# Experts' token lists from rank 3 on: from matrix products in every pass to one scatter through DRAM

## The reference, cut to what matters

```python
top_logit, top_e = lax.top_k(logits, 4)              # logits = rmsnorm(h) @ w_router + b_router
gates = softmax(top_logit)
for each expert e, on the tokens that chose it:
    gate, up = split(x @ w_gate_up[e] + b_gate_up[e])
    act = (clip(up, -7, 7) + 1) * min(gate, 7) * sigmoid(1.702 * min(gate, 7))
    y = act @ w_down[e] + b_down[e]
h = h + sum over the four experts of gates * y
```

## Time and profile before

| | us |
|---|---|
| median of three runs | 2447.67 (2446.9 to 2454.19) |
| the profiled execution | 2456.49 |
| its span, first to last instruction | 2454.7 |
| the 32 passes of the experts | 773.0 to about 2304 |
| one pass, 192 columns / 108 columns | 63.5 / 43.3 |
| PE / DVE / ACT / POOL busy | 2378.4 / 1148.4 / 586.3 / 349.0 |

### The profile page before, as it was taken

The page is one execution under the profiler, slowest core; times in us unless marked ns, Lnnn a source line. Parts: engine busy times, 40 slices in busy tenths (PEclk is TensorE's granted clock), DMA queues, the critical chain, the costliest instruction groups (busy, mean ns, idle before and its releaser), DMA issues. The chain is left out here.

```text
span 2454.7 us, 48279 instructions
## 1 busy us (share of the span) xinstructions
PE 2378.4 (97%) x19277; PEld 2186.8 (89%) x19278; DVE 1148.4 (47%) x1886; ACT 586.3 (24%) x1248; POOL 349.0 (14%) x371
## 2 busy tenths in 40 slices
PE   8999999989996999999999999999999999999898
PEld 6787787688675999999999999999999999999776
DVE  4686816575435223334333434435434334343485
ACT  4434414644321000011011111111111111111265
POOL 0240103262001000110001100101001010010230
PEclk9999996999998999999999999999999999999899
DMA  4131214001526766778888888888888988888652
GB/s 154 66 125 56 95 56 148 27 3 32 193 69 238 285 231 234 249 259 282 288 288 280 296 305 304 304 323 302 315 326 312 321 311 320 313 310 305 211 202 77
DMA packets 123451, 541.02 MB, mean 220 GB/s; under 512 B 15301, under 2 KB 47257, under 8 KB 74169
## 3 DMA queue, kind: packets, MB, share of 16 engines
q1 hardware_dynamic: 106904, 487.45, 56.0%
q0 software_dynamic: 16416, 51.66, 6.2%
HBM read 492.13 MB, written 46.92 MB: 220 GB/s over the span
## 5 line engine op out<-in xcount | busy, mean ns | idle before, releaser
L1960 PE MATMUL ex_psum<-ex_xT,weight_ring_a 128*128 128x134 f32 (+14 forms) x7168 | 896.8, 286 | 4.2 <-DVE ex_xT L1813 3.5
L1960 PEld LDWEIGHTS ex_psum<-ex_xT,weight_ring_a 128*128 128x128 f32 x7168 | 882.0, 191 | 5.0 <-issue 4.3
L2002 PE MATMUL ex_psum<-ex_hT,weight_ring_b 128*128 128x134 f32 (+14 forms) x4096 | 506.0, 286 | 0.0
L2002 PEld LDWEIGHTS ex_psum<-ex_hT,weight_ring_b 128*128 128x128 f32 x4096 | 503.0, 191 | 0.0
L1799 POOL DMA_INDIRECT ex_rows<-xn_dram,ex_list x164 | 155.4, 948 | 1358.9 <-DVE ex_list L1855 1311.7
L1970 DVE TENSOR_SCALAR ex_gate<-ex_psum,bias_gate_up 128x192 f32<-128x192 f32 x256 | 92.6, 403 | 521.4 <-PE ex_psum L1960 515.8
L1974 DVE TENSOR_SCALAR ex_up<-ex_psum,bias_gate_up 128x192 f32<-128x192 f32 x256 | 94.9, 413 | 388.9 <-PE ex_psum L1960 235.7
L1987 ACT ACTIVATE ex_sig<-ex_gate 128x384 f32<-128x384 f32 x128 | 67.0, 523 | 765.8 <-DVE ex_gate L1970 726.9
L2012 ACT ACTIVATE ex_yT<-ex_psum,bias_down 128x192 f32<-128x192 f32 x256 | 83.1, 436 | 503.3 <-PE ex_psum L2002 503.3
L2265 PE MATMUL project_psum<-n_hi,w_in_hi 128*128 128x512 f32 x464 | 186.0, 401 | 2.9 <-DVE n_lo L541 2.9
L2265 PE MATMUL project_psum<-n_lo,w_in_hi 128*128 128x512 f32 x464 | 182.1, 392 | 0.0
(11 more groups left out here) (358 smaller groups left out, 2489.3 us busy)
## 6 DMA issues: line engine op xcount, KB each, us to landing
weight_ring_a<-in_w_gate_up SPq DMA_DIRECT2D x224, 1024.0 KB, 4.8
weight_ring_b<-in_w_down SPq DMA_DIRECT2D x128, 1024.0 KB, 7.1
weight_ring_b<-in_w_gate_up SPq DMA_DIRECT2D x32, 1024.0 KB, 6.9
y_dram<-ex_y SPq DMA_DIRECT2D x80, 192.0 KB
w_in_pieces<-in_w_in SPq DMA_DIRECT2D x29, 512.0 KB, 3.6
y_dram<-ex_y SPq DMA_DIRECT2D x52, 128.0 KB
distances_dram<-qkvT POOLq DMA_DIRECT2D x12, 512.0 KB, 3.0
gla_dist<-distances_dram SPq DMA_DIRECT2D x12, 512.0 KB, 4.3
```

The source lines that it names most:

```text
L1960: mm = pe.matmul(self.ps[:, bank, i * CAP:i * CAP + width], w[:, k, i * P:(i + 1) * P], self.xT[:, k, 0:width], start=(k == 0), stop=(k == ...
L2002: mm = pe.matmul(self.ps[:, bank, first:first + width], w[:, i, j], self.hT[:, k, 0:width], start=(k == 0 and j % 2 == 0), stop=(k == KT - ...
```

## The change

The lists of ranks 0, 1 and 2 (`FIRST_LISTS` = 3) are made as before. For the others:

- `dve_slots` moves to before pass 1. The slot of a token and choice holds its rank and its place.
- A new DRAM tensor `list_dram` has one number per slot. SP zeroes its first part from the blank tile, between the wait for `y_zero` and the store of the blank rows. DVE waits for that zeroing (`lists_zero`) before pass 0, and POOL before its first scatter.
- POOL scatters for each of 8 token tiles and 4 choices 128 numbers (four times the token's number, a constant) to the slots: 32 indirect DMAs. The first 16 stand behind the gather for rank 1, then comes the gather for rank 2, then the other 16, then a wait for all of them and four reads of the whole table with one rank per partition.
- DVE waits for these reads before pass 2 and turns them (`dve_turn_lists`). In each pass from 2 on, a small DVE instruction (`dve_list_by_rank`) takes the place of `dve_list`.
- PE, from pass 2 on, has no list and no fold; DVE has no marks and no spread.
- The loops of the passes are cut at 2 on PE, and into six stretches in place of four on DVE.
- The extra passes for experts with over 192 tokens keep the old way. They are entered only where a count exceeds the capacity.

```diff
+FIRST_LISTS = 3
...
+    k[:, K_ROW:K_ROW + NT] = QUARTERS * (np.arange(NT) * P + i[:, None])
...
+    def dve_list_by_rank(self, dve, x, narrow=False):
+
+        n = BLOCKS_NARROW if narrow else BLOCKS
+        with self.nc.allow_low_precision(reason="row numbers, whole numbers below 2**24"):
+            dve.tensor_scalar(self.list[:, 0:n], self.lists[:, 0:n, bass.ds(x, 1)].rearrange("p b a -> p (b a)"),
+                              self.g.k[:, K_QUARTER:K_QUARTER + 1], None, ALU.add).then_inc(self.listed, 1)
+
+    def pool_scatter(self, pool, tiles):
+
+        g = self.g
+        for t in tiles:
+            for k in range(TOPK):
+                pool.indirect_dma_start(out=g.list_dram, out_offset=bass.IndirectOffsetOnAxis(ap=g.slot[:, t, k:k + 1], axis=0),
+                                        in_=g.k[:, K_ROW + t:K_ROW + t + 1], in_offset=None).then_inc(self.scattered, 16)
+
+    def pool_read_lists(self, pool):
+
+        g = self.g
+        pool.wait_ge(self.scattered, 16 * NT * TOPK)
+        for a in range(QUARTERS):
+            pool.dma_start(self.by_rank[a * SQ:(a + 1) * SQ, :],
+                           g.list_dram[CAP:CAP + E * CAP, :].rearrange("(e n) a -> e (n a)", n=CAP)).then_inc(self.lists_in, 16)
+
+    def dve_turn_lists(self, dve):
+        dve.wait_ge(self.lists_in, 16 * QUARTERS)
+        dve.wait_ge(self.last_zero, 1)
+        dve.transpose(self.lists[:, :, 0:E], self.by_rank[:].rearrange("p (b r) -> p b r", r=SQ)).then_inc(self.lists_turned, 1)
+        dve.wait_ge(self.lists_turned, 1)
...
             sp.wait_ge(x.y_zero, 1)
+            sp.dma_start(g.list_dram[0:Y_FIRST, :].rearrange("(e n) a -> e (n a)", n=CAP),
+                         x.y[0:E + 1].rearrange("p b r -> p (b r)")[:, 0:CAP]).then_inc(x.lists_zero, 16)
...
             x.first_gather(pool)
-            with pool.Fori(0, NARROW - 1) as e:
+            x.gather(pool, 1)
+            pool.wait_ge(x.lists_zero, 16)
+            pool.wait_ge(x.slot_done, 1)
+            x.pool_scatter(pool, range(NT // 2))
+            x.gather(pool, 2)
+            x.pool_scatter(pool, range(NT // 2, NT))
+            x.pool_read_lists(pool)
+            with pool.Fori(2, NARROW - 1) as e:
...
                 for c in range(4):
                     x.pe_gate_up(pe, e, e + 1, c, width)
-                    if c == 0:
-                        x.pe_list(pe, e + 1, 8 * e + 4, narrow_x)
-                    if c == 1:
-                        x.pe_fold(pe, e + 1, narrow_x)
+                    if marks and c == 0:
+                        x.pe_list(pe, e + 1, 8 * e + 4)
+                    if marks and c == 1:
+                        x.pe_fold(pe, e + 1, e + 1)
...
             x.dve_fit(dve)
-            for first, end in ((0, NARROW - 1), (NARROW - 1, NARROW), (NARROW, NARROW + 1), (NARROW + 1, E)):
-                narrow = first + 1 >= NARROW
-                if first == NARROW - 1:
+            dve.memset(x.lists[:, :, E:E + 1], 0.0).then_inc(x.last_zero, 1)
+            dve.wait_ge(x.lists_zero, 16)
+            for first, end in ((0, 1), (1, FIRST_LISTS - 1), (FIRST_LISTS - 1, NARROW - 1), (NARROW - 1, NARROW), (NARROW, NARROW + 1), (NARROW + 1, E)):
+                narrow, marks = first + 1 >= NARROW, first + 1 < FIRST_LISTS
+                if first == 1:
                     x.dve_slots(dve)
+                if first == FIRST_LISTS - 1:
+                    x.dve_turn_lists(dve)
                 with dve.Fori(first, end) as e:
-                    x.dve_find(dve, e + 1, x.expert_at(dve, e + 1, E))
+                    if marks:
+                        x.dve_find(dve, e + 1, x.expert_at(dve, e + 1, E))
...
                         if c == 1:
-                            x.dve_list(dve, e + 1, None, narrow)
+                            if marks:
+                                x.dve_list(dve, e + 1, None)
+                            else:
+                                x.dve_list_by_rank(dve, e + 1, narrow)
```

More of the change, by code:

```diff
@@ L1745, in __init__ @@
         self.list = sb("list", [P, BLOCKS], U32)
+        self.by_rank = sb("lists_by_rank", [P, CAP])
+        self.lists = sb("lists", [P, BLOCKS, E + 1])
         self.spread_a = sb("spread_a", [P, 2, BLOCKS_NARROW], BF16)
@@ L1766, in __init__ @@
         self.y_zero, self.banks_zero = sem("y_zero"), sem("banks_zero")
+        self.lists_zero, self.scattered, self.lists_in, self.lists_turned, self.last_zero = (
+            sem(n) for n in ("lists_zeroed", "lists_scattered", "lists_in", "lists_turned", "last_list_zero"))
         self.first_rows = [sem(f"first_rows_in{b}") for b in range(BLOCKS)]
@@ L1814, in dve_first_turns, with pe_list @@
         turn.then_inc(self.x_turned, 1)
-    def pe_list(self, pe, x, kept, narrow=False):
-        pe.wait_ge(self.marked, x + 1)
-        pe.wait_ge(self.spread, 2 * x)
+    def pe_list(self, pe, i, kept, narrow=False):
+        pe.wait_ge(self.marked, i + 1)
+        pe.wait_ge(self.spread, 2 * i)
         pe.wait_ge(self.yT_kept, kept)
@@ L1824, in pe_list, with dve_spread @@
         mm.then_inc(self.list_summed, 1)
-    def dve_spread(self, dve, x, narrow=False):
-        dve.wait_ge(self.list_summed, x + 1)
-        dve.wait_ge(self.folded, x)
+    def dve_spread(self, dve, i, narrow=False):
+        dve.wait_ge(self.list_summed, i + 1)
+        dve.wait_ge(self.folded, i)
         block = self.g.k[:, K_BLOCK:K_BLOCK + BLOCKS_NARROW]
@@ L1836, in dve_spread, with pe_fold @@
                               self.ps[0:n, self.LIST, 2:4].unsqueeze(2).to_broadcast([n, 2, more]), ALU.mult).then_inc(self.spread, 1)
-    def pe_fold(self, pe, x, narrow=False):
-        pe.wait_ge(self.spread, 2 * x + 2)
+    def pe_fold(self, pe, i, x, narrow=False):
+        pe.wait_ge(self.spread, 2 * i + 2)
         pe.wait_ge(self.listed, x)
@@ L1846, in pe_fold, with dve_list @@
         mm.then_inc(self.folded, 1)
-    def dve_list(self, dve, x, landed, narrow=False):
-        dve.wait_ge(self.folded, x + 1)
+    def dve_list_by_rank(self, dve, x, narrow=False):
[20 more added lines that the diff above has]
+        dve.wait_ge(self.lists_turned, 1)
+    def dve_list(self, dve, i, landed, narrow=False):
+        dve.wait_ge(self.folded, i + 1)
         if landed is not None:
@@ L2162, in passes @@
             def passes(first, end, columns):
-                cuts = sorted({first, end} | {c for c in (NARROW - 1,) if first < c < end})
+                cuts = sorted({first, end} | {c for c in (FIRST_LISTS - 1,) if first < c < end})
                 for lo, hi in zip(cuts, cuts[1:]):
                     if hi == lo + 1:
-                        one_pass(lo, columns, lo + 1 >= NARROW)
+                        one_pass(lo, columns, lo + 1 < FIRST_LISTS)
                     else:
                         with pe.Fori(lo, hi) as e:
-                            one_pass(e, columns, lo + 1 >= NARROW)
+                            one_pass(e, columns, lo + 1 < FIRST_LISTS)
             first = 0
@@ L2227, in _ @@
                         x.dve_gate_up(dve, e, expert, c)
-                        if c == 0:
-                            x.dve_spread(dve, e + 1, narrow)
+                        if marks and c == 0:
+                            x.dve_spread(dve, e + 1)
                         if c == 1:
-                            x.dve_list(dve, e + 1, None, narrow)
+                            if marks:
+                                x.dve_list(dve, e + 1, None)
+                            else:
+                                x.dve_list_by_rank(dve, e + 1, narrow)
                         if c == 2:
@@ L2239, in body @@
                 expert = x.expert_at(dve, e)
-                x.dve_find(dve, n + E + 1, expert)
-                x.dve_spread(dve, n + E + 1)
-                x.dve_list(dve, n + E + 1, x.rows_total_late(n) - 16 * BLOCKS)
+                x.dve_find(dve, n + FIRST_LISTS, expert)
+                x.dve_spread(dve, n + FIRST_LISTS)
+                x.dve_list(dve, n + FIRST_LISTS, x.rows_total_late(n) - 16 * BLOCKS)
                 x.dve_turn_x(dve, n + E + 1, x.rows_total_late(n), 8 * m)
```

16 lines of the change are left out of this document (9 added, 7 removed).

## The result

| | us | runs |
|---|---|---|
| kernel after, median | 2432.37 (2431.79 to 2436.77) | 5 |
| kernel before beside it | 2447.96 (2446.9 to 2454.19) | 5 |
| after / before | 0.9939, 95% interval 0.9926 to 0.9952 | |
| profiled execution of after, its span | 2432.29, 2430.5 | 1 |

The kernel became 0.6% faster, 14.9 us by the ratio (11.8 to 18.1). The forecast was 2432.0.

The account below looks back on a forecast made before the run. PE's queue was taken as the bound (busy 97%). Removed lists 26.0 us, less 7.6 of stall and 2.7 of clock, gave 15.7 off the 2447.67 median: 2432.0 us, range 2420 to 2445.

Parts of the forecast that it names:

- The removal: PE, passes 2 to 31: list matmuls of ranks 3 to 32 go, a gain of 26.0 us.
- The steps for passes 2 to 12: PE, passes 2 to 12: the list costs 1.06 us a pass, 11.7 us in all.
- the late ones: PE, the 14 passes with the narrow list: 0.37 us a pass, 5.2 us in all.
- I let it go together with the list: PE, passes 13 to 17: issue stops vanish with the list, 1.83 us a pass, 9.15 us in all.
- the lower bound: Smallest gain from removing the lists on PE, if the issue stops of passes 13 to 17 stay: 22.2 us.
- The stop in pass 0: PE at the rank 1 list stands still while DVE waits for the zeroing: 7.6 us, bounds 3.2 to 9.5.
- The clock behind it: PE after the stall in pass 0: 5.4 us at half speed, a loss of 2.7 us, bounds 0 to 4.7.
- Slots and marks on DVE: DVE: slot computation (7.3 us) before pass 1 fits idle time, dropped marks were under cover; no cost or gain.
- The scatters: POOL: 32 scatters at 1.25 us each and four reads, lists landing at 910.3, 17.7 us spare; no cost.
- rival C: POOL: scatters to DRAM are slow; from 2.7 us each the whole gain is gone, 2463.6 us at 3.2; chance 0.12.
- A: Pass 0: the zeroing lands in time, no stall and no clock loss, 2421.7 us; chance 0.10.
- B: Pass 0: blank rows hold up the zeroing until about 798, a 17.6 us stall, 2442.0 us; chance 0.12.

Follow-up runs that it names:

- e10: The kernel before, unchanged, profiled once more in one run: 2449.67 us.
- e3: Kernel after with all its additions kept, but every list still made by marks and matrix products, the scattered lists unused: 2456.26 us, 1.0023 of the kernel before.
- e1: Kernel after with DVE's wait for the zeroing moved to its first write into the blank tile: 2426.41 us, 0.9906 of the kernel before.
- e2: Kernel after with SP issuing the zeroing ahead of the four 1024 KB loads: 2424.28 us, 0.9896 of the kernel before.
- e4: Kernel after plus 16 + 4 small one-shape matmuls of constants in passes 2 to 31, without DVE: 2455.41 us, 1.002 of the kernel before.
- e6: Kernel after with all 32 scatters undivided, ahead of rank 2's gather: 2435.53 us, 0.994 of the kernel before.
- e5: Kernel after with every scatter issued twice, the second into an unread table, 64 in all: 2448.83 us, 1.0001 of the kernel before.
- e11: Kernel after plus small matmuls of constants in the wide list's shapes, passes 2 to 31; 2394.53 us, no measure because a slip narrowed the big matmuls.
- e9: Kernel after with both the zeroing issued ahead of the loads and DVE's wait for it made later: 2427.89 us, 0.9909 of the kernel before.
- e8: Kernel before with only the slot computation moved from before pass 18 to before pass 1: 2450.8 us, 0.9999 of the kernel before.

## Why the prediction was right

**What bounds the kernel.** Right: PE's queue set the time. 24.2 us went from span to span: 27.2 in passes 1 to 31, less 7.5 that came back in pass 0. The rest, 4.5, lies almost all ahead of pass 0, which began at 773.0 before and at 768.9 after; without any change it began at 769.3 in e10, so this part is not a gain of the change.

**The removal: the term that was mis-sized.** The steps for passes 2 to 12 (1.06; 1.08 measured) and for the late ones (0.37; 0.40) held. The one that failed is "I let it go together with the list", for the stops of passes 13 to 17. They did go in after, but e3 and e10 show that they had belonged to the one execution of before that was profiled: without a change passes 1 to 31 take 1464.1 us in e10 and 1468.4 in the earlier trace rows's execution, and 1441.2 in after. The change is worth 22.9 us there, not 26.0: the 9.15 us booked for these five passes were 5.4. The 22.2 of the lower bound was nearer. Why the stops were there once is open.

**The stop in pass 0.** The mechanism was right, as e1, e2 and e3 show from three sides. Its size was forecast at 7.6 us; it was 4.09, 4.40, 5.83, 5.83, 8.07 and 8.09 in the six profiled executions that have it, median 5.83. Two things made the difference. Where chunk 0 ran at half clock (after, e4 and e6), PE came 1.7 us later and stood that much less: with a chunk 0 at full clock the stops of after, e6 and e5 would be 5.8 to 6.1 us, those of e4, e3 and e11 7.5 to 8.1. And in these last three the packets of the zeroing end with three late ones, 1.3 to 2.2 us behind the other 30, while in the first three all 33 come within 1 us. After's own stop had both the slow chunk and no late packet: its zeroing had landed by about 782, over 1 us before the load ahead of it, where I had put it 0.9 behind.

The Trainium skill (DMA: Bandwidth & Descriptors, Why a DMA increments its semaphore by 16 and not by 1) states that a transfer from SP uses the largest number of engines, up to 16, that divides its outer dimension, 11 for 33 rows, and that the semaphore is complete when these have landed their data. The traces fit this: in all six executions the last packet of the zeroing ends before the load ahead of it has landed, by 0.2 to 2.5 us, and the three late packets are as many as one of 11 engines would have. No view names a packet's engine, so that isn't shown. The 4.5 us that the prediction worked out by it was nearer to after's 4.09; its own 7.6 was nearer to the stops with late packets.

**The clock behind it.** Forecast 2.7 us lost. Half of the time that PE worked at half clock behind the stop is 1.7 us in after, 1.8 in e3, and at most 3.4 (e11, its stop 8.09), with a median of 2.8: inside the bounds. After 4.09 us of standing still at granted 1.00 the clock was 0.50 for 3.4 us; behind e5's 10.16 us it was 0.50 for 3.57.

**Stop and clock together** were booked at 10.3 us. In the six executions they are 5.8 to 11.5, median 8.9. Pass 0 as a whole, which also holds a slow chunk 0, has a median of 72.95 us in these six and of 65.01 in the seven profiled executions without the stop: 7.9 us. By the ratios of e1, e2 and e9 it is 8.1, 10.5 and 7.4, by that of e3 5.6. So the loss was probably smaller than booked, by some 2 us, though the intervals of e1, e2 and e9 don't exclude the full 10.3; that of e3 (3.2 to 8.1) does.

**Slots and marks on DVE: nothing.** Right within the noise: e8 measured 0.9999 (0.9986 to 1.0012), pass 1 took 63.48 us as before, and 11.24 us of idle time were left.

**The scatters: nothing.** 1.27 us each against 1.25 taken. Their last landed 8.00 us after POOL was through with it, not 2.9, but the four reads took 2.09 us of POOL and not 5.0, the stage began 4 us earlier, and the stop was shorter: turned at 907.66 against a landing forecast at 910.3. The room was 12.9 us and not 17.7. e5 showed the wait behind it where the prediction put it, and that rival C's way of losing the gain is real: with twice the scatters the gain is gone.

**The rivals.** A (no stop) is what e1, e2 and e9 are, and not what after is: 2424.3 to 2427.9 there against A's 2421.7. B (blank rows hold the zeroing up to 798) fell: it had landed by 782. C fell by the scatter's 0.97 us and 0.30 to the next.

**The sum.** 26.0 - 10.3 = 15.7 was booked. By the profiles it is 22.9 - 8.9 = 14.0, or 15.0 with the 7.9 of pass 0 as a whole; the ratio gives 14.9 (11.8 to 18.1). Removal and loss were both taken too high, by 3.1 and by 1.4 to 2.4 us, and this cancelled for the most part: that the sum came so near owes something to luck.

## What to carry to other kernels

A small transfer that an engine waits for belongs ahead of the large ones in its queue, or its wait as late as its data is needed: here that made the gain half as large again or more (0.6% became 0.9 to 1.0% in e1, e2 and e9). A stop seen in one profiled execution is no property of the kernel: before a term is taken from it, look for it in a second execution. And work moved to an engine off the path is free only up to its slack; doubling it, as e5 does, measures both the slack and the price beyond.

## What the runs showed of the hardware

- Small bf16 matmuls of 2 columns with one shape follow each other at 25 ns (16 in 0.40 us); with weights of 128 x 128 and then 128 x 64, and the fold's two shapes, 16 and 4 take 0.61 and 0.25 us; the first matmul behind a change of shape starts 90 to 100 ns after the one before it (e10, e11).
- A scatter of 128 numbers of 4 bytes takes POOL no longer than a gather of 128 rows (0.97 and 0.95 us), but the last of 32 had landed only 8.0 us after POOL was through with it, while weights were loaded; the last of 64 after 4.6.
- A transfer of 33 rows of 768 bytes, issued 0.9 us behind the last of four loads of 1 MB on the same queue, ended 10.6 us after its issue, 2.5 us before that load; issued ahead of them it ended 1.0 us after its issue (after, e2).
- The same kernel ran with five passes of 45.7 us and, on another occasion, of 44.92, with the difference in idle time put down to "issue". No cause was found.
